# Four narrow keys projected once, and exchanged between the halves by identity products

## The chip, the cores and the metric

The kernel runs on one core of one Trainium2 chip. Measured is the device time of one execution, in microseconds (us). TensorE (PE) multiplies, VectorE (DVE), ScalarE (ACT) and GpSimd (POOL) work on elements, and SyncE (SP) issues the transfers. Each engine takes its own instructions in their order and waits for the others by semaphores.

## The reference

Two blocks follow one another, each of two layers, on 256 tokens of 1024 features, all in float32. The change is in the first block's mixing, here cut to what matters:

```python
p = h @ w_in                       # one product, cut into twelve parts
qa, ka, va, qi, ki, wi, qb, kb, vb, qc, kc, vc = split(p)
qa, ka = rope(rms(qa, qn_a)), rope(rms(ka, kn_a))   # 4 query heads, ONE key head of 64
qi, ki = rope(qi), rope(ki)                         # 4 index heads, ONE index key of 64
qc, kc = rope(rms(qc, qn_c)), rope(rms(kc, kn_c))   # 8 query heads, TWO key heads of 64
# branch a: score = sum_h wi_h * relu(qi_h . ki), causal, keep the 64 largest of each row,
#           then softmax attention of qa over ka, va at the kept places
# branch b: stick-breaking attention of qb, kb, vb (4 heads)
# branch c: attention in a window of 128 tokens, with sinks
x = x + g1 * (rms(concat(oa, ob, oc), g_out) @ w_o)
h = rms(x, ln2) * (1 + sc2) + sh2
x = x + g2 * swiglu(h)
```

The four narrow keys are ka, ki and the two heads of kc: 64 columns of w_in each.

## The kernel before

All weights stream in as units of 128 output columns by 1024 inputs (512 KB, in two halves). For each half SP sends it into RAW (room for two units), ScalarE writes its high part WH (`split_high`, L2131), and VectorE (first half, L2392) and POOL (second half, L1735) write the rest, WL. WH and WL hold four units. TensorE then makes the unit in 24 products of 256 columns (`feature_unit`, L1818 to L1820: eight slices of the inputs, three products each) into bank u % 4, ScalarE evicts the bank, and only then splits unit u + 4. SP, ScalarE, VectorE and POOL each have one written-out order of work; a step of one that waits holds up all that stands behind it on that engine.

The input product of a layer of the first block is units x = 0 to 19, and each engine has a loop over x in which other work is hung behind certain units. Units 0 to 3 and 8 to 19 are features by tokens, evicted to F[x] (x < 4) or F[x - 4]; units 4 to 7 are values, tokens by features, made in two pairs (L1863 to L1865). Before the change unit 2 holds ki twice (its 64 columns and the same again), unit 3 the first head of kc twice, unit 8 the second head twice, and unit 9 ka twice. The halves are wanted because the scores are products over 64 rows: the odd heads of a query lie in rows 64 to 127 of F, and need their key in the same rows.

What is hung into the loops, before the change:

- `rotate(r)` on TensorE (L1954) multiplies F[ROPES[r]] by a rotation matrix into bank 4, `cosine` on POOL (L1728) and `rope(r)` on VectorE (L2548, L2551) finish it. There are seven: rotate(0) behind x = 2, rotate(1) (F[2], the index key) behind 5, rotate(2) to (4) behind 12, 14, 16, rotate(5) (F[5], ka) behind 18, rotate(6) behind 19.
- `index_scores(n)` on TensorE (L1964), for token block n, behind x = 7 and x = 9, into banks 5 and 6. n = 1 waits until VectorE has read n = 0. VectorE's `index_terms(n)` (L2573) behind 7 and 9, and `index_sum(n)` (L2581) behind 8 and 11.
- `key_sums(c)` on TensorE (L1927) behind 9 and 10: sums of squares of the normed keys, c = 0 for kc, c = 1 for ka. ScalarE's `key_roots(c)` (first line of it L2162) behind 9 and 11, VectorE's `key_norm(c)` (L2407, L2409, L2413, L2559) behind 10 and 13. rotate(2) waits for key_norm(0).
- `modulate` on TensorE (L1799): the adaptive scales, one step of four products, behind 3, 5, 7, 11, 13 in layer 0 and 5, 9, 13 in layer 1. SP sends the two 512 KB halves of a step (L1647) into a ring of four, between the units' weights.
- `highest()` on VectorE: four rounds of the search for the 64 largest, behind 13, 15, 16, 17 (four more come later).

Behind the loop come the attention's scores (`score`, L2021 and L2025; VectorE's first read of the stick scores is L2639, of the c scores L2660), transposes (L2041) and weighted values (L2053), with modulation steps between them, then the output product and the feed forward.

Of the kernel before, what the change touches and what calls it, by code (L numbers as in the profile page):

```python
# [7 lines left out]
P = 128  # L8
# [35 lines left out]
BESIDE_HALVES = 2 * BESIDE * KC  # L44
BESIDE_FIRST = 2 * (LEAD + 2 * KC)
IN_UNITS = V_UNITS + QK_UNITS
KEY_I, VALUES, QUERY_C, QUERY_A = 2, 4, 10, 14
KEYS = (3, 8, 9)
GAIN_OF = {3: 7, 8: 7, 9: 2, **{QUERY_C + i: 3 for i in range(4)}, QUERY_A: 0, QUERY_A + 1: 0}
ROPES = ((0, 2), (2, 1), (3, 2), (6, 2), (8, 2), (5, 1), (10, 2))  # L50
KEY_ROPES = {2: 1, 5: 2}
HEADS = {"c0": (6, 3, 1, 4, 0), "c1": (8, 4, 2, 6, 64), "a": (10, 5, 0, 0, 128), "b": (12, 14, 3, 2, 256)}
# [88 lines left out]
def build(nc, stream, mods, consts, consts2, par1, par2, lam, ccols, xT, ctxT, outT):  # L141
# [1571 lines left out]
    @block.gpsimd  # L1713
    def _(pool):
        def cosine(l, r):

            at, chunks = ROPES[r]
            if r in KEY_ROPES:
                pool.wait_ge(k_normed, 2 * l + KEY_ROPES[r])
            else:  # L1720
                for u in range(at, at + chunks):
                    evicted(pool, l * PER + (u if u < VALUES else u + V_UNITS))
            if r == 0 and l == 0:
                pool.wait_ge(consts_in, 16)
            if r >= 2:
                pool.wait_ge(rope_done, 7 * l + r - 1)
            cos = const("cos", T)[:, None, :].broadcast_to([P, chunks, T])
            pool.tensor_tensor(RO[:, r % 2, 0:chunks, :], F[:, at:at + chunks, :], cos, ALU.mult).then_inc(cosd, 1)  # L1728

        cut = slice(KC // 2, KC)  # L1730

        def low(u, i=0):

            pool.wait_ge(hi_done, 8 * i + (2 * u + 2))
            pool.tensor_tensor(WL[:, u % 4, cut, :], RAW[:, (2 * u + 1) % 4, :, :],  # L1735
                               WH[:, u % 4, cut, :].bitcast(f32), ALU.subtract).then_inc(lo_done[1], 1)

        def lows(first, end):
            rounds = (end - first) // 4
            if rounds:  # L1740
                with pool.Fori(0, rounds) as i:
                    for u in range(first, first + 4):
                        low(u, i)
            for u in range(first + 4 * rounds, end):
                low(u)

        def hidden(l, first):

            with pool.Fori(0, FF_UNITS // 4) as i:
                for j in range(4):  # L1750
                    low(first + j, i)
                    if j % 2:
                        pool.wait_ge(ffhi, 2 * i + (l * FC + j // 2 + 1))
                        chunk = bass.ds(2 * i + j // 2, 1)
                        pool.tensor_tensor(HID[:, 1, chunk, :], GATE[:, 2:3, :], HID[:, 0, chunk, :].bitcast(f32),  # L1755
                                           ALU.subtract).then_inc(ff_done, 1)


        first = 0
        for l in range(DEPTH):  # L1760
            base, end = l * PER, l * PER + IN_UNITS + 4
            lows(first, base + 4)
            for x in range(IN_UNITS):
                low(base + x + 4)
                for r, after in enumerate((1, 4, 11, 13, 15, 17, 18)):
# [12 lines left out]
    def _(pe):  # L1778
# [109 lines left out]
        def first_layer(l):  # L1888
# [28 lines left out]

            def key_sums(c):

                for x in KEYS[2:] if c else KEYS[:2]:  # L1920
                    evicted(pe, base + x)
                if c:
                    pe.wait_ge(mr_done, 2 * l + 1)
                else:
                    pe.wait_ge(rot_read, 7 * l + 2)
                cut = slice(2, 3) if c else slice(0, 2)
                pe.matmul(PS[:, 4, 0:(2 - c) * T], heads, SQK[:, cut, :], start=True, stop=True).then_inc(ms_done, 1)  # L1927

            def query_sums(chunks):

# [11 lines left out]
            def rotate(r):  # L1942
# [5 lines left out]
                    for u in range(first, first + chunks):  # L1948
                        evicted(pe, base + (u if u < VALUES else u + V_UNITS))
                if r:  # L1950
                    pe.wait_ge(rot_read, 7 * l + r)
# [4 lines left out]

            def index_scores(n):

                pe.wait_ge(rope_done, 7 * l + 2)
                if n:  # L1960
                    pe.wait_ge(index_read, 2 * l + 1)
                for p, h in enumerate(PLACE):
                    r = slice(64 * (h % 2), 64 * (h % 2) + 64)
                    last = pe.matmul(INDEX[:, p, 0:P * (n + 1)], F[r, h // 2, n * P:(n + 1) * P],  # L1964
                                     F[r, KEY_I, 0:P * (n + 1)], start=True, stop=True)
                last.then_inc(index_done, 1)

            steps = iter(range(at + (NORM_STEPS if l else 0), at + QK_STEPS))
            for x in range(IN_UNITS):
                if x in (VALUES, VALUES + 2):  # L1970
                    token_pair(base, 0, x, H1, 0, 2)
                elif x == 0:
                    units_begun([(base + y, H1, T) for y in range(BEGINNING[l])], 2 * l)
                elif x >= BEGINNING[l] and not VALUES < x < VALUES + 4:
                    unit(x)
                if x == 2:
# [2 lines left out]
                    rotate(0)  # L1979
                if x == 5:  # L1980
                    rotate(1)
                if x == 7:
                    index_scores(0)
                if x == 9:
                    key_sums(0)
                    index_scores(1)
                if x == 10:
                    key_sums(1)
                if x in (12, 14, 16, 18, 19):
                    rotate({12: 2, 14: 3, 16: 4, 18: 5, 19: 6}[x])  # L1990
                if x == 15:
                    query_sums(range(QUERY_C, QUERY_C + 4))
                if x == 17:
# [5 lines left out]
            def score(i):  # L1999
# [9 lines left out]
                else:  # L2009
                    pe.wait_ge(exped, 6 * l + i - 3)  # L2010
                if name == "c0":
                    pe.wait_ge(rope_done, 7 * l + 4)
                if name == "c1":
                    pe.wait_ge(rope_done, 7 * l + 5)
                if name == "a":
                    pe.wait_ge(rope_done, 7 * l + 7)
                    pe.wait_ge(sel_done, l + 1)
                if name != "b":
                    m = (SELB if name == "a" else BAND)[:, n, 0:w][:, None, :].broadcast_to([P, 2, w])
# [1 line left out]
                        pe.matmul(banks(n)[:, 2 * half:2 * half + 2, 0:w], IDB, m, start=True, stop=False)  # L2021
                for p, h in enumerate(PLACE):
                    r = slice(64 * (h % 2), 64 * (h % 2) + 64)
                    k = key + h // 2 if name == "b" else key
# [35 lines left out]
            modulate(next(steps))  # L2060
            score(2)
            score(3)
            pe.wait_ge(rot_read, 7 * (l + 1))
            pe.wait_ge(qs_read, l + 1)
            for s in steps:
                modulate(s)
# [318 lines left out]
    def _(dve):  # L2385
# [148 lines left out]
        def first_layer(l):  # L2534
# [7 lines left out]
            def rope(r):  # L2542
# [4 lines left out]
                dve.wait_ge(rot_done, 7 * l + r + 1)  # L2547
                dve.tensor_tensor(SN[:, r % 2, 0:chunks, :], rotated, turned_by, ALU.mult).then_inc(rot_read, 1)  # L2548
                dve.wait_ge(rot_read, 7 * l + r + 1)
                dve.wait_ge(cosd, 7 * l + r + 1)  # L2550
                dve.tensor_tensor(F[:, first:first + chunks, :], RO[:, r % 2, 0:chunks, :], SN[:, r % 2, 0:chunks, :],  # L2551
                                  ALU.add).then_inc(rope_done, 1)

            def key_norm(c):

                cut, to = (slice(2, 3), slice(5, 6)) if c else (slice(0, 2), slice(3, 5))
                dve.wait_ge(rx_done, 2 * l + c + 1)
                refine(YK[:, cut, :], VK[:, cut, :])
                dve.tensor_tensor(F[:, to, :], F[:, to, :], YK[:, cut, :], ALU.mult).then_inc(k_normed, 1)  # L2559

            def index_weights():

# [48 lines left out]
            for x in range(IN_UNITS):  # L2611
# [3 lines left out]
                if x == 5:  # L2615
                    rope(1)
                    index_weights()
                if x == 7:
                    index_terms(0)
                if x == 8:  # L2620
                    index_sum(0)
                if x == 9:
                    index_terms(1)
                if x == 10:
                    key_norm(0)
                if x == 11:
# [234 lines left out]
def _weights(a):  # L2861
# [11 lines left out]
    for l in range(DEPTH):  # L2873
        w = a["w_in"][l]
        cuts = np.cumsum([256, 64, 64, 256, 64, 4, 256, 256, 256, 512, 128])
        qa, ka, va, qi, ki, wi, qb, kb, vb, qc, kc, vc = np.split(w, cuts, axis=1)
        put(np.concatenate([qi, ki, ki, kc[:, :64], kc[:, :64]], 1))
        put(np.concatenate([_padded(np.concatenate([vc, va, wi], 1), 256), vb], 1))
        put(np.concatenate([kc[:, 64:], kc[:, 64:], ka, ka, qc, qa, qb, kb], 1))
# [56 lines left out]
def _parameters(a):  # L2936
# [7 lines left out]
    for l in range(DEPTH):  # L2944
# [4 lines left out]
        put(p1, PAR1, l, "gain", np.concatenate([qa, qa, ka, qc, qc, qc, qc, kc, kc], 1))  # L2949
# [38 lines left out]
```

## Time and profile before

| | |
|---|---|
| three timed runs | 2347.58, 2354.19, 2355.84 us (median 2354.19) |
| the profiled execution | 2350.35 us, its span 2348.6 us |
| TensorE busy, weight loads | 2226.4 us (95%), 1936.4 us (82%) |
| VectorE, ScalarE, POOL busy | 1284.9 (55%), 1119.0 (48%), 755.6 us (32%) |
| DMA | 328.47 MB, mean 140 GB/s |
| mean granted clock of TensorE | 0.986 |

The first column of a row of the trace is the start of the instruction, counted from the start of the span, or of a run of like instructions, the second how long it took or they took together. In brackets stands how long the engine had been idle, and what ended that. A single product of 256 columns is shown with 0.28 us, but they are pipelined, and in a unit one starts every 0.12 us. A float32 product that is not split beforehand shows as two instructions. The input product of layer 0 lies at 35 to 115 us of the span, that of layer 1 at 430 to 503 us.

### The profile page before, as it was taken

Reading aid. Unit: us, or ns where it says so; the run is one execution under the profiler, and the core shown is the slowest. Engines: PE = TensorE matmul, PEld = TensorE weight load, DVE = VectorE, ACT = ScalarE, POOL = GpSimd, SP = SyncE. Lnnn points to the kernel's source line nnn. Section 1 sums busy time; section 2 is a strip of 40 time slices with the busy share of each in tenths; the row PEclk is TensorE's granted clock in tenths of the full one; section 3 lists DMA queues with packets and bytes.
Section 4 is the critical chain, followed back from the end, with each engine's and each line's share of the span. In section 5 each row is a group of like instructions: output and inputs, shape, how many; then the busy total and the mean of one; then the engine's idle time right before and its main releaser. Section 6 shows DMA issues by size and latency. Waiting matters only on the chain.

```text
span 2348.6 us, 41122 instructions
## 1 busy us (share of the span) xinstructions
PE 2226.4 (95%) x14780; PEld 1936.4 (82%) x14780; DVE 1284.9 (55%) x2274; ACT 1119.0 (48%) x2324; POOL 755.6 (32%) x563
## 2 busy tenths in 40 slices
PE   7989988889999899999999999999989999999998
PEld 4859888767899798878879669888879999787998
DVE  3767767586435654551243765354456564437663
ACT  3565444455455534542354663233334565647553
POOL 2504675331465321112322002212213225221443
PEclk9999999999999999999999999999999999999999
DMA  8665888757766332213222112223323335222554
GB/s 301 225 220 170 279 274 294 230 184 237 253 188 188 121 108 72 63 59 94 85 77 79 48 35 81 90 72 93 95 72 119 99 107 174 86 82 71 159 167 142
DMA packets 159781, 328.47 MB, mean 140 GB/s; under 512 B 17696, under 2 KB 21024, under 8 KB 159520
## 3 DMA queue, kind: packets, MB, share of 16 engines
q1 hardware_dynamic: 159504, 325.80, 44.0%
q8 instruction: 89, 1.46, 0.3%
q0 software_dynamic: 144, 0.85, 0.1%
q14 instruction: 44, 0.36, 0.1%
HBM read 325.53 MB, written 1.05 MB: 139 GB/s over the span
## 4 chain that ended last, share of the span: by engine, by line
PE 64%; issue 16%; POOL 7%; DVE 5%; DMA 4%; ACT 2%; SPq 1%; POOLq 0%; DVEq 0%; ACTq 0%
PE PS L1818 13%; PE PS L1819 13%; PE PS L1820 13%; POOL WL L1735 6%; PE PS L1863 4%; PE PS L1865 4%; PE PS L1864 4%; DMA RAW<-stream 3%; POOL AR L1755 2%; PE PS L702 2%; PE PS L682 1%; ACT WH L2131 1%; DVE WL L2392 1%; PE PS L716 1%; PE PS L718 1%
## 5 line engine op out<-in xcount | busy, mean ns | idle before, releaser
L1735 POOL TENSOR_TENSOR WL<-RAW,WH 128x512 fp32r<-128x512 f32 x468 | 671.9, 1437 | 1519.9 <-ACT WH L2131 1370.0
L1818 PE MATMUL PS<-AR,WH 128*128 128x256 f32 (+1 forms) x2632 | 859.2, 326 | 13.4 <-issue 6.9
L1819 PE MATMUL PS<-AR,WH 128*128 128x256 f32 (+1 forms) x2632 | 844.0, 321 | 0.0
L1820 PE MATMUL PS<-AR,WL 128*128 128x256 f32 (+1 forms) x2632 | 843.9, 321 | 0.0
L2131 ACT ACTIVATE WH<-RAW 128x512 fp32r<-128x512 f32 x908 | 537.2, 627 | 418.6 <-DMA RAW<-stream 241.4
L2392 DVE TENSOR_TENSOR WL<-RAW,WH 128x512 fp32r<-128x512 f32 x468 | 402.2, 859 | 509.4 <-ACT WH L2131 507.6
L1818 PEld LDWEIGHTS PS<-AR,WH 128*128 128x128 f32 x2632 | 496.4, 189 | 72.2 <-issue 23.3
L1819 PEld LDWEIGHTS PS<-AR,WH 128*128 128x128 f32 x2632 | 496.6, 189 | 41.4 <-issue 2.4
L1820 PEld LDWEIGHTS PS<-AR,WL 128*128 128x128 f32 x2632 | 496.4, 189 | 40.1
L1863 PE MATMUL PS<-WH,AR 128*128 128x256 f32 x768 | 219.3, 286 | 0.0
L1865 PE MATMUL PS<-WH,AR 128*128 128x256 f32 x768 | 216.3, 282 | 0.0
L1864 PE MATMUL PS<-WL,AR 128*128 128x256 f32 x768 | 216.2, 282 | 0.0
L1863 PEld LDWEIGHTS PS<-WH,AR 128*128 128x128 f32 x768 | 144.7, 188 | 3.3 <-issue 3.0
L1864 PEld LDWEIGHTS PS<-WL,AR 128*128 128x128 f32 x768 | 144.7, 188 | 0.7 <-issue 0.5
L1865 PEld LDWEIGHTS PS<-WH,AR 128*128 128x128 f32 x768 | 144.6, 188 | 0.0
L1880 PE MATMUL PS<-AR,WH 128*128 128x256 f32 x352 | 100.4, 285 | 12.5 <-issue 10.4
L1881 PE MATMUL PS<-AR,WH 128*128 128x256 f32 x352 | 99.0, 281 | 0.0
L1882 PE MATMUL PS<-AR,WL 128*128 128x256 f32 x352 | 99.0, 281 | 0.0
L1003 ACT ACTIVATE WORK<-PS 128x512 f32<-128x512 f32 (+1 forms) x48 | 23.5, 489 | 122.9 <-PE PS L1820 122.5
L1880 PEld LDWEIGHTS PS<-AR,WH 128*128 128x128 f32 x352 | 66.2, 188 | 15.3 <-issue 14.6
L2494 DVE SCALAR_TENSOR_TENSOR WORK<-WORK 128x1024 f32<-128x1024 f32 x48 | 72.0, 1500 | 0.0
L1065 ACT ACTIVATE WORK<-PS,BC,QN 128x512 f32<-128x512 f32 (+1 forms) x96 | 66.9, 705 | 8.9 <-DVE BC L1463 8.9
(307 smaller groups left out, 2950.9 us busy)
## 6 DMA issues: line engine op xcount, KB each, us to landing
RAW<-stream SPq DMA_DIRECT2D x936, 256.0 KB, 3.1
WORK<-mods SPq DMA_DIRECT2D x144, 512.0 KB, 5.5
C<-consts SPq DMA_DIRECT2D x1, 1088.0 KB, 7.4
XX<-xT SPq DMA_DIRECT2D x1, 1024.0 KB, 10.0
XX<-ctxT SPq DMA_DIRECT2D x1, 1024.0 KB, 5.9
outT<-XX SPq DMA_DIRECT2D x1, 1024.0 KB, 4.8
C<-consts POOLq DMA_DIRECT2D x1, 832.0 KB, 6.9
WORK<-lam SPq DMA_DIRECT2D x1, 256.0 KB, 6.3
```

Of the source, the lines that this page charges most:

```text
L1735: pool.tensor_tensor(WL[:, u % 4, cut, :], RAW[:, (2 * u + 1) % 4, :, :], WH[:, u % 4, cut, :].bitcast(f32), ALU.subtract).then_inc(lo_don ...
L1818: pe.matmul(out, WH[:, u % 4, k, :], moving[:, 0, k, :], start=(k == 0), stop=False)
L1819: pe.matmul(out, WH[:, u % 4, k, :], moving[:, 1, k, :], start=False, stop=False)
L1820: last = pe.matmul(out, WL[:, u % 4, k, :], moving[:, 0, k, :], start=False, stop=(k == KC - 1))
L1863: pe.matmul(out, still[:, 0, k, cut], WH[:, both, k, :], start=(k == 0), stop=False)
L1864: pe.matmul(out, still[:, 0, k, cut], WL[:, both, k, :], start=False, stop=False)
L1865: last = pe.matmul(out, still[:, 1, k, cut], WH[:, both, k, :], start=False, stop=(k == KC - 1))
L1880: pe.matmul(PS[:, b, 0:T], WH[:, u % 4, k, :], HID[:, 0, kk, :], start=(kk == 0), stop=False)
L1881: pe.matmul(PS[:, b, 0:T], WH[:, u % 4, k, :], HID[:, 1, kk, :], start=False, stop=False)
L1882: last = pe.matmul(PS[:, b, 0:T], WL[:, u % 4, k, :], HID[:, 0, kk, :], start=False, stop=(kk == FC - 1))
L2131: act.activation(WH[:, u % 4, cut, :], RAW[:, g % 4, :, :], ACT.Copy).then_inc(hi_done, 1)
L2392: dve.tensor_tensor(WL[:, u % 4, cut, :], RAW[:, 2 * u % 4, :, :], WH[:, u % 4, cut, :].bitcast(f32), ALU.subtract).then_inc(lo_done[0], 1)
```

## The change

The units of the four keys become two: unit 2 holds ki in its lower 64 columns and ka in its upper, unit 3 the two heads of kc. Units 8 and 9 have no weights of their own any more: their place in the stream is kept, filled with zeros, and sent, split and waited for as before, but TensorE makes them by two products with the identity, which put the upper half of F[3] (later F[2]) into the lower rows of the bank and the reverse. ScalarE evicts them to F[4] and F[5]. F[2] is swapped behind its rotation, which turns ki and ka at once, so the rotation of F[5] goes (six are left, `TURNS`), and the last comes behind x = 18. The scores take for each head the tile that has its key in the right rows.

```diff
-KEYS = (3, 8, 9)
-ROPES = ((0, 2), (2, 1), (3, 2), (6, 2), (8, 2), (5, 1), (10, 2))
+KEYS = (3, 2)
+SWAPPED = {8: 3, 9: 2}
+ROPES = ((0, 2), (2, 1), (3, 2), (6, 2), (8, 2), (10, 2))
+TURNS = len(ROPES)
+INDEX_KEYS = (2, 5)
...
             def key_sums(c):
-                for x in KEYS[2:] if c else KEYS[:2]:
-                    evicted(pe, base + x)
+                evicted(pe, base + KEYS[c])
+                squares = SQK[:, c, :]
                 if c:
                     pe.wait_ge(mr_done, 2 * l + 1)
+                    second = heads[:, 64:65].broadcast_to([P, P])
+                    pe.matmul(PS[:, 4, 0:T], second, squares, start=True, stop=True).then_inc(ms_done, 1)
+                    return
+                pe.wait_ge(rot_read, TURNS * l + 2)
+                pe.matmul(PS[:, 4, 0:T], heads, squares, start=True, stop=True)
+                for half in range(2):
+                    other = heads[:, 64 - 64 * half:128 - 64 * half]
+                    last = pe.matmul(PS[64 * half:64 * half + 64, 4, T:2 * T], other, squares, start=True, stop=True)
+                last.then_inc(ms_done, 1)
+
+            def swap(x):
+                u = unit_wait(base, 0, x)
+                if x == 8:
+                    evicted(pe, base + SWAPPED[x])
                 else:
-                    pe.wait_ge(rot_read, 7 * l + 2)
-                cut = slice(2, 3) if c else slice(0, 2)
-                pe.matmul(PS[:, 4, 0:(2 - c) * T], heads, SQK[:, cut, :], start=True, stop=True).then_inc(ms_done, 1)
+                    pe.wait_ge(rope_done, TURNS * l + 2)
+                for half in range(2):
+                    other = ident[:, 64 - 64 * half:128 - 64 * half]
+                    last = pe.matmul(PS[64 * half:64 * half + 64, u % 4, 0:T], other, F[:, SWAPPED[x], :],
+                                     start=True, stop=True)
+                last.then_inc(unit_done, 1)
...
             def index_scores(n):
-                pe.wait_ge(rope_done, 7 * l + 2)
+                evicted(pe, base + 9)
...
-                                     F[r, KEY_I, 0:P * (n + 1)], start=True, stop=True)
+                                     F[r, INDEX_KEYS[h % 2], 0:P * (n + 1)], start=True, stop=True)
...  TensorE's loop over x
+                elif x in SWAPPED:
+                    swap(x)
...
-                if x == 7:
-                    index_scores(0)
                 if x == 9:
                     key_sums(0)
+                if x == 10:
+                    index_scores(0)
+                    key_sums(1)
+                if x == 11:
                     index_scores(1)
-                if x == 10:
-                    key_sums(1)
-                if x in (12, 14, 16, 18, 19):
-                    rotate({12: 2, 14: 3, 16: 4, 18: 5, 19: 6}[x])
+                if x in (12, 14, 16, 18):
+                    rotate({12: 2, 14: 3, 16: 4, 18: 5}[x])
...  VectorE's loop over x
-                if x == 7:
-                    index_terms(0)
-                if x == 8:
-                    index_sum(0)
-                if x == 9:
-                    index_terms(1)
                 if x == 10:
                     key_norm(0)
+                    index_terms(0)
                 if x == 11:
+                    index_sum(0)
+                    index_terms(1)
+                if x == 12:
                     index_sum(1)
                 if x == 13:
                     key_norm(1)
-                if x in (12, 14, 16, 18, 19):
-                    rope({12: 2, 14: 3, 16: 4, 18: 5, 19: 6}[x])
+                if x in (12, 14, 16, 18):
+                    rope({12: 2, 14: 3, 16: 4, 18: 5}[x])
```

VectorE's key_norm(1) becomes two products on 64 rows each in place of one on 128, and branch a's scores wait for it directly.

## Rows read from the trace of the kernel before

**Rows 1.** The page, busy us (share of the span) x instructions.

```profile
PE 2226.4 (95%) x14780; PEld 1936.4 (82%) x14780; DVE 1284.9 (55%) x2274; ACT 1119.0 (48%) x2324; POOL 755.6 (32%) x563
```

**Rows 2.** Chain of waits in layer 0: start us, us, what.

```profile
74.28 7.18 DMA RAW<-stream
...
81.54 0.64 ACT WH L2131
...
86.93 0.70 DVE WORK L2559
87.67 1.12 PE PS L1954 x2
```

**Rows 3.** Chain of waits in layer 1.

```profile
467.36 0.59 ACT WORK L2162
...
474.34 1.69 DVE WORK L2559
476.07 1.12 PE PS L1954 x2
...
499.90 0.43 PE PS L1954 x2
```

**Rows 4.** Timeline of TensorE, layer 0: start us, us, engine, line, operation.

```profile
68.37 0.38 PE L1818 MATMUL PS<-AR,WH 128*128 128x256 f32 x1
...
74.16 1.02 PE L1927 MATMUL PS<-WORK,C 128*128 128x512 f32 x2
75.11 1.14 PE L1964 MATMUL PS<-WORK 64*128 64x256 f32 x8
76.19 0.39 PE L1818 MATMUL PS<-AR,WH 128*128 128x256 f32 x1
...
82.52 1.06 PE L1799 MATMUL PS<-WORK,CA 128*32 128x512 f32 x8
83.52 0.39 PE L1818 MATMUL PS<-AR,WH 128*128 128x256 f32 x1
...
95.51 0.59 PE L1954 MATMUL PS<-WORK,C 128*128 128x512 f32 x1
```

**Rows 5.** Timeline of ScalarE and VectorE, layer 0.

```profile
76.59 0.69 ACT L2162 ACTIVATE WORK<-PS,EPSC 128x512 f32<-128x512 f32 x1
...
70.54 1.11 DVE L2573 TENSOR_SCALAR WORK<-PS,COL 128x128 f32<-128x128 f32 x4
...
87.54 0.69 DVE L2392 TENSOR_TENSOR WL<-RAW,WH 128x512 fp32r<-128x512 f32 x1
88.14 2.01 DVE L2581 TENSOR_REDUCE WORK<-WORK 128x256 f32<-128x1024 f32 x1
```

**Rows 6.** Stretches: us, busy us (x) of five engines, PEclk, DMA share, GB/s.

```profile
416.00:418.20 2.20, 2.20 (x18) 2.08 (x18) 2.20 (x4) 1.27 (x3) 1.29 (x1) 1.00 0.79 231
418.40:424.20 5.80, 0.00 (x0) 0.00 (x0) 3.10 (x6) 1.81 (x3) 2.52 (x2) 0.74 0.95 320
424.30:427.60 3.30, 3.30 (x12) 1.44 (x16) 1.07 (x3) 2.39 (x5) 0.90 (x1) 0.50 0.55 187
```

**Rows 7.** Timeline of SP and ScalarE, layer 0.

```profile
83.61 0.81 SPq L1647 DMA_DIRECT2D WORK<-mods  x2
...
89.59 1.20 ACT L2131 ACTIVATE WH<-RAW 128x512 fp32r<-128x512 f32 x2 [2.18 <-DMA RAW<-stream]
```

**Rows 8.** Timeline of VectorE, then of TensorE, behind unit 19 of layer 0.

```profile
116.31 0.68 DVE L2548 TENSOR_TENSOR WORK<-PS,C 128x512 f32<-128x512 f32 x1
...
118.01 1.81 DVE L2639 SCALAR_TENSOR_TENSOR WORK<-PS,C 128x512 f32<-128x512 f32 x2
...
121.80 1.22 DVE L2660 TENSOR_REDUCE COL<-PS 128x4 f32<-128x1024 f32 x1
...
118.75 0.39 PE L2021 MATMUL PS<-WORK 128*128 128x256 bf16 x2 [0.55 <-DVE WORK L2639]
...
120.42 1.14 PE L2025 MATMUL PS<-WORK 64*128 64x256 f32 x8
```

More of the change, by code:

```diff
@@ L46 @@
 IN_UNITS = V_UNITS + QK_UNITS
-KEY_I, VALUES, QUERY_C, QUERY_A = 2, 4, 10, 14
-KEYS = (3, 8, 9)
-GAIN_OF = {3: 7, 8: 7, 9: 2, **{QUERY_C + i: 3 for i in range(4)}, QUERY_A: 0, QUERY_A + 1: 0}
-ROPES = ((0, 2), (2, 1), (3, 2), (6, 2), (8, 2), (5, 1), (10, 2))
-KEY_ROPES = {2: 1, 5: 2}
-HEADS = {"c0": (6, 3, 1, 4, 0), "c1": (8, 4, 2, 6, 64), "a": (10, 5, 0, 0, 128), "b": (12, 14, 3, 2, 256)}
+VALUES, QUERY_C, QUERY_A = 4, 10, 14
+KEYS = (3, 2)
+SWAPPED = {8: 3, 9: 2}
+GAIN_OF = {2: 8, 3: 7, **{QUERY_C + i: 3 for i in range(4)}, QUERY_A: 0, QUERY_A + 1: 0}
+ROPES = ((0, 2), (2, 1), (3, 2), (6, 2), (8, 2), (10, 2))
+TURNS = len(ROPES)
+KEY_ROPES = {2: 1}
+INDEX_KEYS = (2, 5)
+HEADS = {"c0": (6, (3, 4), 1, 4, 0), "c1": (8, (4, 3), 2, 6, 64), "a": (10, (5, 2), 0, 0, 128),
+         "b": (12, 14, 3, 2, 256)}
 SCORED = [(g, n) for g in ("b", "c0", "c1", "a") for n in range(2)]
@@ L1725, in cosine @@
             if r >= 2:
-                pool.wait_ge(rope_done, 7 * l + r - 1)
+                pool.wait_ge(rope_done, TURNS * l + r - 1)
             cos = const("cos", T)[:, None, :].broadcast_to([P, chunks, T])
@@ L1764, in _ @@
                 low(base + x + 4)
-                for r, after in enumerate((1, 4, 11, 13, 15, 17, 18)):
+                for r, after in enumerate((1, 4, 11, 13, 15, 17)):
                     if x == after:
@@ L1950, in rotate @@
                 if r:
-                    pe.wait_ge(rot_read, 7 * l + r)
+                    pe.wait_ge(rot_read, TURNS * l + r)
                 if r in (2, 3, 4):
@@ L2011, in score @@
                 if name == "c0":
-                    pe.wait_ge(rope_done, 7 * l + 4)
+                    pe.wait_ge(rope_done, TURNS * l + 4)
                 if name == "c1":
-                    pe.wait_ge(rope_done, 7 * l + 5)
+                    pe.wait_ge(rope_done, TURNS * l + 5)
                 if name == "a":
-                    pe.wait_ge(rope_done, 7 * l + 7)
+                    pe.wait_ge(rope_done, TURNS * l + 6)
+                    pe.wait_ge(k_normed, 2 * l + 2)
                     pe.wait_ge(sel_done, l + 1)
@@ L2023, in score @@
                     r = slice(64 * (h % 2), 64 * (h % 2) + 64)
-                    k = key + h // 2 if name == "b" else key
+                    k = key + h // 2 if name == "b" else key[h % 2]
                     last = pe.matmul(banks(n)[:, p, 0:w], F[r, first + h // 2, n * P:(n + 1) * P], F[r, k, 0:w],
@@ L2062, in first_layer @@
             score(3)
-            pe.wait_ge(rot_read, 7 * (l + 1))
+            pe.wait_ge(rot_read, TURNS * (l + 1))
             pe.wait_ge(qs_read, l + 1)
@@ L2546, in rope @@
                 rotated = PS[:, 4, 0:chunks * T].rearrange("p (a b) -> p a b", a=chunks)
-                dve.wait_ge(rot_done, 7 * l + r + 1)
+                dve.wait_ge(rot_done, TURNS * l + r + 1)
                 dve.tensor_tensor(SN[:, r % 2, 0:chunks, :], rotated, turned_by, ALU.mult).then_inc(rot_read, 1)
-                dve.wait_ge(rot_read, 7 * l + r + 1)
-                dve.wait_ge(cosd, 7 * l + r + 1)
+                dve.wait_ge(rot_read, TURNS * l + r + 1)
+                dve.wait_ge(cosd, TURNS * l + r + 1)
                 dve.tensor_tensor(F[:, first:first + chunks, :], RO[:, r % 2, 0:chunks, :], SN[:, r % 2, 0:chunks, :],
@@ L2554, in key_norm @@
             def key_norm(c):
-                cut, to = (slice(2, 3), slice(5, 6)) if c else (slice(0, 2), slice(3, 5))
+                cut = slice(2, 3) if c else slice(0, 2)
                 dve.wait_ge(rx_done, 2 * l + c + 1)
                 refine(YK[:, cut, :], VK[:, cut, :])
-                dve.tensor_tensor(F[:, to, :], F[:, to, :], YK[:, cut, :], ALU.mult).then_inc(k_normed, 1)
+                if c:
+                    for half, f in enumerate((5, 2)):
+                        rows = slice(64 * half, 64 * half + 64)
+                        last = dve.tensor_tensor(F[rows, f, :], F[rows, f, :], YK[rows, 2, :], ALU.mult)
+                else:
+                    last = dve.tensor_tensor(F[:, 3:5, :], F[:, 3:5, :], YK[:, cut, :], ALU.mult)
+                last.then_inc(k_normed, 1)
             def index_weights():
@@ L2876, in _weights @@
         qa, ka, va, qi, ki, wi, qb, kb, vb, qc, kc, vc = np.split(w, cuts, axis=1)
-        put(np.concatenate([qi, ki, ki, kc[:, :64], kc[:, :64]], 1))
+        put(np.concatenate([qi, ki, ka, kc], 1))
         put(np.concatenate([_padded(np.concatenate([vc, va, wi], 1), 256), vb], 1))
-        put(np.concatenate([kc[:, 64:], kc[:, 64:], ka, ka, qc, qa, qb, kb], 1))
+        put(np.concatenate([np.zeros((D, len(SWAPPED) * P), np.float32), qc, qa, qb, kb], 1))
         put(a["w_o"][l])
@@ L2948, in _parameters @@
         qa, ka, qc, kc = (twice(a[n][l]) for n in ("qn_a", "kn_a", "qn_c", "kn_c"))
-        put(p1, PAR1, l, "gain", np.concatenate([qa, qa, ka, qc, qc, qc, qc, kc, kc], 1))
+        one_ka = np.concatenate([np.ones(64, np.float32), a["kn_a"][l]])[:, None]
+        put(p1, PAR1, l, "gain", np.concatenate([qa, qa, ka, qc, qc, qc, qc, kc, one_ka], 1))
         put(p1, PAR1, l, "gout", _column(a["g_out"][l].reshape(-1)))
```

## The prediction

> **What bounds the kernel now.** I read the page's busy shares first. TensorE is busy 95% of the span [rows 1], so taking work from TensorE looks like time won, one for one. That is an average over stages, so I read the chain of waits next, inside the stage that the change touches: the 20 units of the input product in each of the two layers of the first block. There the chain is not TensorE's. In layer 0 it goes from a weight transfer (74.28, 7.18 us) that VectorE's low half of unit 12 had freed the slot for, to ScalarE's split of unit 14, then VectorE's key norm, whose last product starts at 86.93, and only then to TensorE, whose rotate(2) starts at 87.67 [rows 2]. In layer 1 it is ScalarE's key root (467.36), the same key norm, and rotate(2) at 476.07 [rows 3]. TensorE reached rotate(2) about 1 us too early both times. So the start of rotate(2) is pinned in both layers by transfers, ScalarE and VectorE, and what TensorE does before it (units 8 and 9 among it) is slack. What matters is which work stands before and behind that pin in the queues.
>
> **Removed.** Per layer two units of 24 products: from the first product of unit 8 (68.37) to the key sum that follows unit 9 (74.16) are 5.79 us, 2.90 each [rows 4]. Also one rotation of 256 columns: 0.43 us of the chain at 499.90 [rows 3], part of it under its neighbours; I take 0.3, bounds 0 and 0.43. The bytes streamed stay the same, since the two units' weights are still sent, split and waited for.
>
> **Added on TensorE.** Two swaps of two 64-column products, and three products for the key sums in place of one. The trace shows no such swap. The index scores of the second block of tokens (75.11 to 76.19, four products of 256 columns on half the rows, 1.08 us) bound a swap from above; below, it can't be less than nothing. Between 0.25 (half of a key sum of 512 columns, 0.95, halved again) and 1.08, I take 0.5, as half the index scores' products. The key sums get dearer by 0.3 to 0.8. Together about 1.5 us, ahead of the pin, so they cost nothing as long as slack is left there. There is: before, the same stretch held 5.79 us more. The rest of that cover: ScalarE evicts the swaps as it evicted the units, its squares of one key moved ahead to unit 2 (under 0.4 us, beside transfers that it waits for), and it reaches the root of the first keys only behind the split of unit 13, so at about 76.6 as before [rows 5].
>
> **Moved, and here I see the cost.** Before, index_scores(0), VectorE's index_terms(0) and index_scores(1) all stood ahead of the key norm. Now VectorE does, in this order, the low half of unit 14, key_norm(0), index_terms(0); and TensorE does unit 10, index_scores(0), the second key sum, unit 11, index_scores(1), the modulation step, unit 12, rotate(2). index_scores(1) overwrites the banks that index_terms(0) reads, and waits for it. So it now waits for the key norm too, and unit 12, which ran before the pin, runs behind it.
>
> When is TensorE there? In layer 0 the root of the keys reads the sums at 76.6 to 77.3 [rows 5], so the second key sum is at 77.3 and unit 11 ends about 80.6. In layer 1 the same reading starts at 467.36 and is over about 468.0 [rows 3], so unit 11 ends about 471.2. Now index_terms(0): after the key norm VectorE took its next instruction at 87.54, and these four instructions took 1.11 us at 70.54 [rows 5], so they end at 88.65, and with the 0.05 us that rotate(2) stood behind its releaser index_scores(1) starts at 88.7. TensorE idles some 8 us. In layer 1 the norm ends at 476.02 [rows 3], the terms at 477.05, the scores start at 477.1: 6 us idle.
>
> Behind that, in layer 0: scores 1.08 us, modulation step 1.00 (82.52 to 83.52), unit 12 2.90 [rows 4]. 88.7 + 4.98 = 93.7 for rotate(2), against 87.67: **+6.0 us**. Layer 1 has no modulation step there: 477.1 + 3.98 = 481.1 against 476.07: **+5.0 us**.
>
> **The clock.** TensorE stood still from 418.4 to 424.2, and then ran 3.3 us at a granted clock of 0.50, the 1.2 GHz level, where 2.2 us before the stop it had 1.00 [rows 6]. Half pace for 3.3 us loses 1.65 us. Both new stalls are as long, and what follows them is dense and on the path: **+1.6 us in each layer**, bounds 0 (if the clock holds) and 1.7. The shorter stops that come earlier (for the swap's eviction, and for the root) may lower it too; that slows unit 11 by up to 1.6, within the 6 to 8 us of idle time.
>
> **Behind rotate(2)** TensorE's order is as before, less the small rotation: **-0.3 us in each layer**. VectorE and the queues must follow. SP sends the modulation halves of unit 15 and then unit 16's weights only when the step at unit 11 has freed a slot (83.61, right behind 83.52), and ScalarE got unit 16's weights at 89.59, 6.0 us later [rows 7]. The step now ends about 92.4, so the weights come about 98.4. VectorE takes their low half (to 99.8), index_sum(1) (a reduction like that of 2.01 us at 88.14 [rows 5], and a sum) and then frees the rotation's bank with its first product at about 102.9. TensorE's rotate(3) stood 7.8 us behind rotate(2) (87.67 to 95.51 [rows 2, 4]), so it now comes at 93.7 + 1.6 + 7.8 = 103.1. That is almost no slack; I count 0, bounds 0 and 4 us. POOL's low half of unit 16 follows VectorE's and is wanted only two units later. In layer 1 no modulation stands at unit 11, so unit 16's weights wait for no step there, and the slack is larger.
>
> **The tail of the stage.** Before, the last rotation came after unit 19, and VectorE did its two products (from 116.31) before it took the stick scores at 118.01 [rows 8]. Now that rotation comes after unit 18, and VectorE goes on 1.70 us earlier against the end of unit 19. TensorE gives back less. Its rotation goes from between unit 19 and the stick scores, but these wait for the eviction of unit 19 (0.3 us is left of it); then comes a modulation step; then its wait of 0.55 us for VectorE at 118.75 goes. So the second c scores, which started at 120.42 and ran 1.14 us, come 0.85 earlier, and VectorE, which read them at 121.80, 0.24 after their end [rows 8], comes 1.1 earlier. From there VectorE's scans set the pace: **-1.1 us in each layer**, bounds 0 and -1.7.
>
> **Sum.** Layer 0: 6.0 + 1.6 - 0.3 - 1.1 = 6.2. Layer 1: 5.0 + 1.6 - 0.3 - 1.1 = 5.2. Together +11.4 us (0.48%). The feed forward behind it has its transfers tied to slots that TensorE frees, so I expect the shift to stay. The profiled execution took 2350.35 us (span 2348.6), which gives 2361.8. The median of the three timed runs is 3.8 us above it, which gives 2365.6. I say 2364.
>
> **Rivals.** (a) TensorE is the bound after all. "Perfetto Trace Analysis" of the Trainium skill (Identifying the Most-Contended Engine) says to take the engine with the highest occupancy, and to optimize it first. By that rule the removed units come through. Worked out from rows: 2 x (5.8 + 0.3 - 1.5) = 9 us, and 2 us of tail: 11 faster, 2341. For it speak the 95% [rows 1]; against it the two chains [rows 2, 3]. It is one mechanism: VectorE would have to be through index_terms(0) before TensorE is through unit 11, at 80.6 and 471.2, which needs weights of unit 14 and a key root some 6 to 8 us earlier. The sign turns where that product of VectorE comes 5.7 us earlier than I have it.
> (b) The stall comes, but the clock is granted again at once or never falls: 2361.8 - 3.2 = 2358.6, or 2360 to 2362 on the median's side.
> (c) The late request of unit 16's weights leaves VectorE late at the next rotation in layer 0, or its selection rounds and sums, now bunched, are late for others: 3 to 6 us more, 2367 to 2370.
> (d) Unit 14's transfer and the root come some 3 us earlier in both layers, now that TensorE frees units 8 and 9 sooner: half of the shift is left, about 2357 to 2359. Against it: that transfer was issued the moment VectorE had unit 12's low half [rows 2], which itself waited for a transfer and not for TensorE.
>
> **Chances.** Forecast 0.50, (a) 0.09, (b) 0.11, (c) 0.17, (d) 0.13. Range 2353 to 2372: all but (a) and the end of (c). Half a per cent is 11.8 us, and is about what a measurement of this kernel can tell from no change. My sum sits just at it, so the forecast's half is shared nearly evenly; (c) is above, (b) and (d) within. That gives faster 0.08, same 0.45, slower 0.47.
>
> **What would show it.** In the profile after: index scores of the second block waiting 5 to 8 us on VectorE's index terms in both layers; key_norm(0) ending at the same 87.6 and 476.0; rotate(2) no longer waiting, and starting near 95.3 and 482.7; granted clock 0.5 for 3 us behind the stall; VectorE's stick products starting less late than TensorE's unit 19. I am wrong if unit 14's weights land well before 81.5, if TensorE has no stop before the second index scores, or if the shift at the end of layer 0 is not in the total.

## The result, and the profile after

The changed kernel took 2358.05 us (median of 20 runs, 2352.57 to 2364.8), the kernel before 2347.68 us (20 runs, 2343.43 to 2355.84). The ratio is 1.0043, with a 95% interval of 1.0033 to 1.0053: some 10 us slower (7.7 to 12.4). The profiled execution took 2361.46 us, its span is 2359.7 us. In these 20 runs the kernel before has a median 6.5 us below that of the three shown ahead of the prediction, so the difference can be compared, and the absolute time less well.

TensorE does less work and is less busy, and the kernel is slower. The first part of the profile's page says only this much:

```profile
PE 2224.0 (94%) x14704; PEld 1930.9 (82%) x14704; DVE 1275.3 (54%) x2272; ACT 1116.3 (47%) x2322; POOL 756.5 (32%) x561
```

The chain of waits shows where it happened. Layer 0 first (start us, us, what; the lines have moved: L1986 is index_scores, L2604 index_terms, L1976 rotate, L2417 VectorE's low half, L1803 the modulation step, L2156 ScalarE's split):

```profile
74.33 5.47 DMA RAW<-stream
...
79.89 0.64 ACT WH L2156
...
80.56 0.69 DVE WL L2417
81.25 0.61 DVE WORK L2432
...
85.93 1.12 DVE WORK L2604 x4
87.05 0.14 issue
87.19 1.78 PE PS L1986 x8
88.97 1.93 PE PS L1803 x8
...
91.71 5.62 DMA RAW<-stream
...
98.77 1.97 DVE WORK L2612
...
102.81 1.10 PE PS L1976 x2
```

Before, the same chain went from the key norm straight to rotate(2) at 87.67 [rows 2]. Now it goes on through the index terms (85.93) to the second index scores, and then, as the modulation step behind them releases SP, to the weights of unit 16 and rotate(3) at 102.81. In layer 1:

```profile
474.55 0.64 ACT WH L2156
...
480.64 1.13 DVE WORK L2604 x4
481.76 0.14 issue
481.90 2.08 PE PS L1986 x8
...
488.37 0.86 PE PS L1976 x2
```

And TensorE's timeline, with its two stops at the second index scores, the swaps (L1947) and the new key sums (L1932, L1935, L1929):

```profile
67.38 1.08 PE L1947 MATMUL PS<-WORK,C 128*64 128x256 f32 x8
68.39 0.70 PE L1932 MATMUL PS<-WORK,C 128*128 128x256 f32 x2
69.02 0.65 PE L1935 MATMUL PS<-WORK,C 128*64 128x256 f32 x4
69.61 0.39 PE L1822 MATMUL PS<-AR,WH 128*128 128x256 f32 x1
...
74.47 0.72 PE L1986 MATMUL PS<-WORK 64*128 64x128 f32 x8 [1.76 <-ACT WORK L2257]
77.22 1.11 PE L1929 MATMUL PS<-WORK,C 128*128 128x256 f32 x2 [2.03 <-ACT WORK L2187]
...
87.19 1.78 PE L1986 MATMUL PS<-WORK 64*128 64x256 f32 x8 [4.90 <-DVE WORK L2604]
88.90 1.93 PE L1803 MATMUL PS<-WORK,CA 128*32 128x512 f32 x8
...
102.81 0.67 PE L1976 MATMUL PS<-WORK,C 128*128 128x512 f32 x1 [1.10 <-DVE WORK L2573]
...
481.90 2.08 PE L1986 MATMUL PS<-WORK 64*128 64x256 f32 x8 [4.89 <-DVE WORK L2604]
```

The reader is to see two things: the gaps in brackets (4.90 and 4.89 us, both released by the index terms), and that the same index scores which took 1.08 us before [rows 4] now take 1.7 and 2.0. The granted clock says why (columns as in rows 6; the first two stretches are of layer 1, the stop and what follows it, the last is what follows the stop in layer 0):

```profile
477.10:481.80 4.70, 0.00 (x0) 0.00 (x0) 4.63 (x8) 2.92 (x7) 2.81 (x3) 0.82 0.64 234
481.90:485.20 3.30, 3.30 (x14) 2.54 (x15) 3.12 (x6) 0.00 (x0) 0.16 (x1) 0.50 0.45 148
...
87.20:90.50 3.30, 3.30 (x16) 1.24 (x16) 3.16 (x7) 0.00 (x0) 0.15 (x1) 0.55 0.00 0
```

### The profile page after: what moved, and what is told of

Same layout as the page of the kernel before. It is cut to its first block, busy times and chain, and to the rows that moved or that the text cites. A ratio compares the mean times of both kernels' runs of the same rounds, so it can differ in the third digit from the quotient of the medians.

```text
span 2359.7 us, 40966 instructions
## 1 busy us (share of the span) xinstructions
PE 2224.0 (94%) x14704; PEld 1930.9 (82%) x14704; DVE 1275.3 (54%) x2272; ACT 1116.3 (47%) x2322; POOL 756.5 (32%) x561
## 3 DMA queue, kind: packets, MB, share of 16 engines
q1 hardware_dynamic: 159504, 325.80, 42.9%
## 4 chain that ended last, share of the span: by engine, by line
PE 65%; issue 16%; POOL 7%; DVE 5%; DMA 4%; ACT 2%; SPq 1%; POOLq 0%; DVEq 0%; ACTq 0%
PE PS L1822 13%; PE PS L1824 13%; PE PS L1823 13%; POOL WL L1739 5%; PE PS L1867 4%; PE PS L1869 4%; PE PS L1868 4%; DMA RAW<-stream 3%; PE PS L706 2%; PE PS L686 1%; POOL AR L1759 1%; ACT WH L2156 1%; DMA WORK<-mods 1%; PE PS L720 1%; PE PS L722 1%
## 5 line engine op out<-in xcount | busy, mean ns | idle before, releaser
L2156 ACT ACTIVATE WH<-RAW 128x512 fp32r<-128x512 f32 x908 | 535.7, 626 | 414.5 <-DMA RAW<-stream 221.4
L2417 DVE TENSOR_TENSOR WL<-RAW,WH 128x512 fp32r<-128x512 f32 x468 | 396.1, 846 | 522.0 <-ACT WH L2156 520.1
```

Of the source, the lines that this page charges most:

```text
L2156: act.activation(WH[:, u % 4, cut, :], RAW[:, g % 4, :, :], ACT.Copy).then_inc(hi_done, 1)
L2417: dve.tensor_tensor(WL[:, u % 4, cut, :], RAW[:, 2 * u % 4, :, :], WH[:, u % 4, cut, :].bitcast(f32), ALU.subtract).then_inc(lo_done[0], 1)
```

## The experiments

Theory A is the prediction's: the places in the queues cost the time (index_scores(1), and behind it unit 12, stand behind VectorE's key norm). Theory B: the removed units had given the next weights time to arrive, and TensorE now starves for them. Each kernel was timed over several rounds beside the kernel before, and profiled. The last two columns are worked out from each profile: from TensorE's first product of the layer's unit 0 to its first attention scores (the whole stage of the input product), layer 0 and layer 1.

| kernel | ratio to before | 95% interval | layer 0, us | layer 1, us |
|---|---|---|---|---|
| before, two profiles | 1 | | 80.10, 80.05 | 73.95, 74.25 |
| changed, two profiles | 1.0043, 1.0044 | 1.0033 to 1.0053, 1.0029 to 1.0060 | 88.43, 87.19 | 81.50, 81.62 |
| order only | 1.0072 | 1.0058 to 1.0085 | 87.93 | 79.98 |
| terms early | 0.9995 | 0.9983 to 1.0007 | 82.59 | 73.49 |
| scores late | 0.9996 | 0.9986 to 1.0005 | 80.62 | 75.17 |
| short transfers | 1.0046 | 1.0032 to 1.0059 | 87.34 | 78.92 |
| stop filled | 1.0045 | 1.0027 to 1.0062 | 86.42 | 78.81 |
| reordered | 0.9975 | 0.9963 to 0.9988 | 76.53 | 73.86 |
| reordered, short | 0.9968 | 0.9954 to 0.9982 | 74.69 | 72.66 |

### The order alone

```diff
 TensorE's loop of the kernel BEFORE (all units and rotations kept)
-                if x == 7:
-                    index_scores(0)
                 if x == 9:
                     key_sums(0)
-                    index_scores(1)
                 if x == 10:
+                    index_scores(0)
                     key_sums(1)
+                if x == 11:
+                    index_scores(1)
 and VectorE's as in the change: key_norm(0), index_terms(0) behind 10, and so on
```

> The kernel before, with units 8 and 9 still full units and all seven rotations, but with the index work in the new order: index_scores(0) behind unit 10, index_scores(1) behind unit 11, and on VectorE index_terms(0) behind key_norm(0). Theory A (the new order is what costs: index_scores(1) and unit 12 now stand behind the key norm): 6.0 and 5.0 us of stall and work behind it in the two layers, 1.5 us of half clock in each, about 1 us at the next rotation of layer 0, and nothing of the 0.6 to 1 us that each layer gets back at the tail: 12 to 16 us slower than before, so more than the changed kernel's 10. In the profile index_scores(1) waits 4 to 6 us for VectorE's index terms in both layers. Theory B (the removed units took away the time in which the next weights came, and TensorE starves for them): the order alone costs under 4 us, and the stall before index_scores(1) is short.

Measured 2363.3 us against 2347.1 of before: 13.6 to 20 us slower, the upper half of what theory A allowed or a little above it, and far from B's 4. The stop is there, in layer 0 of this kernel (and in layer 1: 4.93 us):

```profile
86.60 2.08 PE L1964 MATMUL PS<-WORK 64*128 64x256 f32 x8 [4.95 <-DVE WORK L2573]
```

So the new order is enough to make the loss, with no unit removed. Against this kernel the changed one is 0.28% better (1.0072 to 1.0044): so much the removed units, the dropped rotation and the shorter tail brought together. Where is not shown: up to the first scores its two stages (87.93 and 79.98 us) were about as long as those of the changed kernel or shorter, and the tails are worth 2 us.

### Index terms ahead of the key norm

```diff
-                if x == 10:
-                    key_norm(0)
-                    index_terms(0)
-                if x == 11:
-                    index_sum(0)
-                    index_terms(1)
+                if x == 9:
+                    index_terms(0)
+                    index_sum(0)
+                if x == 10:
+                    key_norm(0)
+                if x == 11:
+                    index_terms(1)
```

> The changed kernel with index_terms(0) and index_sum(0) taken on VectorE behind the low half of unit 13, ahead of the low half of unit 14 and the key norm. Theory A: index_scores(1) finds its banks read and does not wait; rotate(2) is again set by the key norm or by TensorE's own work, within 0.5 us of where it stood before in both layers; with the tail's 0.6 to 1 us and the dropped rotation the kernel is 0 to 3 us faster than before, 10 to 13 faster than the changed one. Theory B: the stall moves to unit 11 or 12, and the time stays within 4 us of the changed kernel.

Measured 2345.3 us against 2347.1, ratio 0.9995: the loss is gone by index_terms(0), with its sum, moved on VectorE. TensorE no longer waits for the index terms:

```profile
83.28 1.14 PE L1986 MATMUL PS<-WORK 64*128 64x256 f32 x8
84.35 1.06 PE L1803 MATMUL PS<-WORK,CA 128*32 128x512 f32 x8
...
88.31 0.59 PE L1976 MATMUL PS<-WORK,C 128*128 128x512 f32 x1
```

rotate(2) comes 53.14 us behind the layer's first product (52.25 before, 58.94 in the changed kernel). That is 0.9 later than before, not within 0.5 as expected: two short stops earlier (2.77 and 0.47 us, at the first index scores and the second key sum) make TensorE late by itself. In layer 1 it comes 0.75 earlier than before (45.30 against 46.05).

### The second index scores behind rotate(2)

```diff
                 if x in (12, 14, 16, 18):
                     rotate({12: 2, 14: 3, 16: 4, 18: 5}[x])
-                if x == 11:      (it stood ahead of these two lines)
+                if x == 12:
                     index_scores(1)
 VectorE: index_terms(1) behind rope(2), index_sum(1) behind 13
```

> The changed kernel with VectorE's key norm and index_terms(0) left where they are, but TensorE takes index_scores(1) behind rotate(2), and VectorE index_terms(1) behind the products of that rotation. Theory A: unit 12 runs while VectorE does the key norm, so rotate(2) starts where it stood before; then index_scores(1) waits up to 1 us and takes 1.1: 1 slower to 2 us faster than before, and no stop of TensorE over 2 us between unit 11 and rotate(3). Theory B: no gain over the changed kernel.

Measured 2345.3 us, ratio 0.9996. Here VectorE's order ahead of rotate(2) was left alone, and TensorE's changed instead; the result is the same. rotate(2) starts when the key norm lets it, 51.0 and 45.7 us behind the layer's first product (before: 52.25 and 46.05):

```profile
82.20 1.07 PE L1803 MATMUL PS<-WORK,CA 128*32 128x512 f32 x8
...
86.79 1.12 PE L1976 MATMUL PS<-WORK,C 128*128 128x512 f32 x2 [0.48 <-DVE WORK L2589]
87.92 1.14 PE L1986 MATMUL PS<-WORK 64*128 64x256 f32 x8
```

Two different repairs of the one order, each worth some 11 us: theory A stands, B falls.

### Fewer bytes for the empty units

```diff
+                if isinstance(v, int) and v < DEPTH * PER and v % PER in SWAPPED:
+                    few = slice(half * KC // 2, half * KC // 2 + 1)
+                    sp.dma_start(RAW[:, g % 4, 0:1, :], stream[v, :, few, :]).then_inc(raw_full[g % 4], 16)
+                    continue
```

> The changed kernel, in its order, with the two zero units of each layer sent as an eighth of their bytes (64 KB in place of 512 KB each; what lies in the buffer besides is split as before and not used). Theory A, in which the pin is set by transfers: unit 14's weights land up to 3 us earlier in each layer (0.9 MB less at about 300 GB/s), the key norm and all behind it come 1 to 3 us earlier per layer: 2 to 6 us faster than the changed kernel, still slower than before by 4 to 8. If transfers do not set the pin: no change, 10 us slower than before.

What was sent is a quarter and not an eighth: 64 KB for each half of 256 KB, eight such transfers in all; the queue carried 324.23 MB, in the changed kernel 325.80. So it is 0.8 MB less in each layer, not 0.9.

Measured 2356.5 us, ratio 1.0046: no change in the total, a miss for what I had made of theory A. The chain of layer 0 shows how:

```profile
68.01 3.69 DMA RAW<-stream
...
71.78 0.64 ACT WH L2160
...
73.17 6.94 DMA RAW<-stream
...
80.20 0.64 ACT WH L2160
```

Unit 12's weights took 3.7 us instead of 4.7, but unit 14's 6.9 instead of 5.5, and they landed at 80.20 instead of 79.89. Counted from the layer's first product that is 45.0 us in both. In layer 0 the pin is a chain of slots (each transfer starts when VectorE's low half frees its place), not of the bytes of units 8 and 9, which were sent 15 to 19 us earlier. What sets the 4.5 to 7.2 us of unit 14's transfer there is not settled; two halves of a modulation step are sent just ahead of it, but no run takes them away.

In layer 1 the forecast was not missed: unit 14's weights came 39.1 us behind the first product (39.9 and 39.7 in two profiles of the changed kernel), index_terms(0) began at 44.1 (45.9 and 45.7), and rotate(2) stood at 50.9 (53.5 and 53.6). The stage was 2.6 us shorter (table), and the total does not show it.

### The stop filled with products

```diff
+                if x == 11:
+                    u = unit_wait(base, 0, 12)
+                    for n in range(FILL):       # FILL = 36
+                        pe.matmul(PS[:, u % 4, 0:T], WH[:, u % 4, n % KC, :], H1[:, 0, n % KC, :], start=True, stop=True)
```

> The changed kernel with 36 more products of 256 columns (4.3 us at full clock, unit 12's high part times the inputs, into unit 12's bank, which unit 12 then overwrites) on TensorE between unit 11 and index_scores(1), in both layers: they fill the stop without lengthening it. Theory A (the clock after the stop costs 1.5 us a layer): the granted clock stays 1.0 behind the stop, index_scores(1) takes 1.1 us instead of 1.7, rotate(2) comes 1.2 to 1.6 us earlier in each layer, 2 to 3.5 us faster than the changed kernel. If the clock's price is not on the path, no change. If the stop is shorter than the filling, it is slower than the changed kernel by up to 2 us.

The clock behind the stop stayed up, and the scores took 1.07 us again, from start to next start (the stretch has the columns of rows 6):

```profile
86.70:90.00 3.30, 3.29 (x26) 2.13 (x27) 3.16 (x6) 0.00 (x0) 0.18 (x1) 1.00 0.04 5
```

```profile
81.62 4.43 PE L2004 MATMUL PS<-AR,WH 128*128 128x256 f32 x36
86.71 1.14 PE L1987 MATMUL PS<-WORK 64*128 64x256 f32 x8 [0.65 <-DVE WORK L2609]
87.78 1.06 PE L1804 MATMUL PS<-WORK,CA 128*32 128x512 f32 x8
```

rotate(2) came 56.85 us behind the layer's first product, against 58.94 and 58.42 in two profiles of the changed kernel: 1.6 to 2.1 earlier, and the stage of layer 1 was 2.7 shorter. The clock's part is clearest from the start of the second index scores to rotate(2): 5.02 us in layer 0 and 4.03 in layer 1, against 6.60 and 7.73, and 6.30 and 6.70, in the two profiles of the changed kernel. So half clock cost 1.6 to 2.7 us a layer, not 1.5. In the time of the whole kernel it can't be seen: 1.0045 (1.0027 to 1.0062) beside 1.0044 (1.0029 to 1.0060) for the changed kernel on the same chip. Its two stages were 4.7 and 3.6 us shorter than in those two profiles, 0.15 to 0.20%, where each interval is 0.17% wide to either side. And in its profile the 2.0 us won in the stage of layer 0 were gone again when layer 1 began (434.82 us, 434.70 in the first profile of the changed kernel). So the clock's price is shown in the stage, and open in the total.

### The changed kernel again, and the kernel before again

> The changed kernel once more, beside the others of this call on the same chip: 10 us (0.3 to 0.55%) slower than before, whatever theory holds. It is here as the measure for the kernel with the filled stop.

2358.4 us, ratio 1.0044, as before. The stop before the second index scores was 3.31 us in layer 0 and 5.72 in layer 1 in this profile (4.90 and 4.89 in the first), and the clock behind it again 0.50.

> The kernel before once more, for one profile: how much its stretches vary from execution to execution. If the 2 to 3 us that the changed kernel gained in layer 0's feed forward (232.1 us from its first unit to layer 1 before, 229.6 and 228.3 in two profiles of the changed kernel) come from chance, this one lies between 226 and 231 us too. If the change causes them, it lies at 231 to 233. The stage of the input product to the first scores stays within 0.5 us of 80.1 and 74.0.

One profile: 2349.08 us. Its two stages are the same to 0.3 us (table). The feed forward of layer 0, to the start of layer 1, took 230.8 us, against 232.1 in the first profile of before and 229.6 and 228.3 in the two of the changed kernel. That is the edge between the two expectations and does not decide. The other profiles say more: the feed forward took 225.7 to 230.4 us in the eight profiles of kernels with the merged keys, and 230.8 to 232.1 in the three with the old ones (the two of before and the order alone). So the change seems to shorten it, by some 3.5 us in the mean; by what, no run shows. The attention of layer 0 differed by 2 us between the two profiles of one kernel (51.4 and 53.5).

### A better order

```diff
 TensorE
-                if x == 10:
+                if x == 11:
                     index_scores(0)
                     key_sums(1)
-                if x == 11:
+                if x == 12:
                     index_scores(1)
 ScalarE
                     key_roots(0)
-                if x == 11:
                     key_roots(1)
 VectorE
+                if x == 9:
+                    index_terms(0)
+                    key_norm(0)
                 if x == 10:
-                    key_norm(0)
-                    index_terms(0)
+                    index_sum(0)
                 if x == 11:
-                    index_sum(0)
                     index_terms(1)
+                    rope(2)
...                  (and rope(2) no longer behind 12)
```

> The changed kernel with its work put in another order: TensorE takes units 10 and 11 at once, then index_scores(0), the second key sum, unit 12, index_scores(1); ScalarE takes both key roots behind the split of unit 13; VectorE takes index_terms(0) and key_norm(0) ahead of the low half of unit 14, and rope(2) ahead of that of unit 16. Theory A (the loss and the pin are places in the queues, and the removed units are gained once nothing waits there): rotate(2) starts at 82 to 84 us in layer 0 instead of 93.8 (before: 87.7), 8 to 14 us faster than the changed kernel altogether, up to 8 faster than before with 3 of them likely given back at later weights. Theory B (weights arrive too late for TensorE whatever the order): no better than before, with TensorE waiting for low halves of units 12 to 16.

Measured 2342.6 us against 2347.4, ratio 0.9975 (0.9963 to 0.9988): 3 to 9 us faster than before, 16 faster than the changed kernel (expected 8 to 14). rotate(2) starts at 83.45, within the 82 to 84 expected. The key norm now stands ahead of unit 14's low half, so it no longer waits for that transfer, and the units run through:

```profile
77.75 0.67 PE L1929 MATMUL PS<-WORK,C 128*128 128x256 f32 x2 [1.20 <-ACT WORK L2187]
78.34 1.07 PE L1803 MATMUL PS<-WORK,CA 128*32 128x512 f32 x8
...
82.38 1.14 PE L1986 MATMUL PS<-WORK 64*128 64x256 f32 x8
83.45 1.12 PE L1976 MATMUL PS<-WORK,C 128*128 128x512 f32 x2
```

Of the gain of some 6 us the stages show 3.6, all in layer 0. Layer 1 has none over the kernel before (73.86): there a wait of 2.0 us for VectorE at rotate(4) took its place. One rival is untested: the kernel before, with units 8 and 9 kept as they were, was not run in this order. So it is shown that the order makes the changed kernel faster than before, but not how much of that the removed units give and how much the order would have given without them.

> As e7_reordered, and the two zero units of each layer sent and split to an eighth only. The run with the short transfers alone moved nothing. Theory A: with the queues in order each engine and the transfers have some 2 us more in hand per layer, 0 to 3 us faster than e7_reordered. Theory B: if weights are what it waits for, this one gains over e7_reordered by more than 3 us.

The same order, with the empty units sent and split to a quarter (again not an eighth): 2338.5 us against 2347.4, ratio 0.9968 (0.9954 to 0.9982), the fastest of all, but its interval overlaps that of the run above. The medians lie 4.1 us apart and the ratios 1.6, so the total does not tell theory A's 0 to 3 from theory B's more than 3. The stages were 1.8 and 1.2 us shorter.

## Why the prediction was right, step by step

- **The pin.** Right. The key norm ended 46.0 us behind the first product of layer 1 before (476.03) and after (480.71); in layer 0 52.2 and 51.2. I had it unmoved; it was 1.0 us earlier in layer 0, as unit 14's weights were there at 79.89 where before it was 81.54 [rows 2], or 45.0 and 46.1 us behind the layer's first product.
- **Added work.** Right: two swaps took 1.01 us (67.38 to 68.39), 0.5 each as estimated, and the first key sums 1.22 instead of 0.95 [rows 4]. All of it was ahead of the pin.
- **The wait of index_scores(1) for index_terms(0).** Right in place and releaser. The stop was 4.9 us in both layers where I had 8 and 6, mainly because unit 11 ended later (82.3): the two stops before it (1.76 and 2.03 us) had brought the clock down (0.53 from 77.2 to 79.2), which I had allowed for. The start of the scores counts, not the length of the stop: 87.19, or 0.95 us earlier against the first product than my 88.7.
- **Scores, modulation step and unit 12 behind the pin, and the clock.** The work was right, the clock's price too low. rotate(2) came 6.7 us later than before against the layer's first product in layer 0 (7.6 forecast, 1.0 of the difference being the earlier pin) and 7.4 later in layer 1 (6.6 forecast). Half pace for 3.3 us was there, clock 0.55 and 0.50, but in layer 1 it lasted longer: from the scores to rotate(2) it took 6.30 us where I had 3.98 + 1.6. In the second profile it was 7.73 in layer 0 (4.98 + 1.6 forecast) and 6.70 in layer 1. So the clock cost 1.6 to 2.8 us a layer, and in three of four cases more than my upper bound of 1.7.
- **The dropped rotation.** Wrong by 0.5 us a layer. The 0.3 did not come: from the rotation behind unit 18 to the first scores it took 4.43 us in both layers, where before it was 4.23. The rotation of 512 columns now stands there in place of the small one, and TensorE waits 0.56 us for the eviction of unit 19.
- **VectorE ready at rotate(3).** I counted nothing, with "almost no slack", and rival (c) as its price. TensorE waited 1.10 us there, which made up for the earlier pin. A piece of rival (c), then, not all of it.
- **The tail.** The second c scores were read 7.3 us later than before where the first stick scores were 8.3 later: 1.0 given back, 1.1 forecast. VectorE at the end of the stage of layer 0 (compare rows 8):

```profile
124.30 1.90 DVE L2668 SCALAR_TENSOR_TENSOR WORK<-PS,C 128x512 f32<-128x512 f32 x2
...
128.57 1.23 DVE L2689 TENSOR_REDUCE COL<-PS 128x4 f32<-128x1024 f32 x1 [0.32 <-PE PS L2050]
```

- **The sum.** 11.4 us forecast; 10.4 between the medians. Up to the first scores the two stages lost 15.8 us in the first profile and 14.6 in the second (table, against 80.1 and 74.1), less 2 for the tails: 12.6 to 13.8. So the terms of the stages were 1 to 2.5 us too small together. The 2 to 3 us between that and 10.4 came back elsewhere, perhaps in layer 0's feed forward; what it was is open. That the sum came so close is thus in part luck: I had expected the shift to stay whole. The time itself, 2358.05 where I said 2364, is lower mostly because the three timed runs that I started from lay 6.5 us above the median of 20. By the time alone (b), with its 2358.6, would fit better; the traces decide against it.
- **What can be told apart.** I took half a per cent for about the least that can be told from no change. Twenty runs of each gave 0.43% with 0.10% to either side, clear of no change.
- **Rivals.** (a), that TensorE's 95% make it the bound, fell: TensorE had 76 instructions less and the kernel was slower. "Perfetto Trace Analysis" of the Trainium skill (Identifying the Most-Contended Engine) says to optimize first the engine with the highest occupancy, and to judge TensorE's headroom by, among others, the busy share of its weight loads; with 82% that too is above every other engine here. Taken as a forecast, the rule would have had the removed units come through. Here the most occupied engine was not what set the start of rotate(2), and the measurement decides. (b) fell (clock 0.50). (d) fell, but for its 1 us in layer 0.

## What to carry to other kernels

Before taking work from the busiest engine, find in the chain of waits the point that another engine pins, and count only what is removed behind it. A step that is moved past such a point, in any queue, costs all that stands behind it there; here a 1.1 us step of VectorE, put behind a key norm instead of ahead of it in each of two layers, was worth 11 us. When a removal gives nothing, try the order again with the work gone: the same change with its steps in another order was 0.25% faster than before instead of 0.43% slower. And a gain of 2 to 5 us that a stage shows in one profile need not be in the total: twice here it was not.

## What the runs showed of the hardware

In layer 0 unit 14's weights did not come sooner when 0.8 MB were taken out of the queue 15 to 19 us ahead of them: 6.94 us from issue to landing in the run with short transfers, 5.47 and 4.45 in two profiles of the changed kernel. In layer 1 they came 0.6 to 0.8 us sooner. And 36 products put into a stop of 4.9 us kept TensorE's clock at 1.00, where 3.3 us at 0.50 to 0.55 followed without them, at no cost that the runs could tell.
